# Zeros for the fill of two DRAM tables come from the norm rows' buffer, and one table gets only its extra blocks filled

## The chip, the cores and the metric

The kernel runs on one core of a Trainium2 chip. The metric is the device time of one execution in microseconds (us), smaller being better.

## The reference, cut to what matters

The program is a two-layer encoder on 512 rows of 1024 numbers. Layer 0 mixes tokens with a bidirectional gated DeltaNet, layer 1 with latent attention; each mixer is followed by a layer norm, a mixture of 16 experts of which every token uses two, and another layer norm.

```python
for i in range(DEPTH):
    y = gated_deltanet(x) if i % 2 == 0 else latent_attention(x)
    x = layernorm(ALPHA * x + y, ln1_g[i], ln1_b[i])
    y = grouped_moe(x)        # each token: top 2 experts of its best group
    x = layernorm(ALPHA * x + y, ln2_g[i], ln2_b[i])
```

The change concerns two internal DRAM tables that the expert mixture uses. Each has 26 blocks of 96 rows of 1024 float32: one block for each of the 16 experts, and EXTRA = 10 blocks for tokens that don't fit in an expert's first 96 places.

## The kernel before, in words

The stages run one after the other: the DeltaNet (`delta_net`), the mixture of layer 0, the norm with attention, the mixture of layer 1, the last norm. All engines meet in a barrier between two stages. Within a stage each engine runs its own list of instructions in order, and semaphores tie them.

The DeltaNet goes through 8 head groups ("heads" below, i = 0 to 7). Head 0 is prepared ahead; then one loop body per head does this on the engines: TensorE projects the next head (`wqkv`, the weights of head i+1) while VectorE builds the inverse of a 128x128 triangular matrix per tile (products into `X`, updates of `TU` at L999). Then come the four steps over the chunks of the sequence, in both directions, at L1043 to L1083 (`for st in range(4)`): TensorE makes the chunk's state and output, VectorE takes them over, and TensorE needs VectorE's new state `St` for the next step. In step 0 VectorE copies the first state out of PSUM (L1070) and the first output into `o` (L1079), so `o` is overwritten from here on. After the steps the output is gated and multiplied by `wo`, and added to `res` (L1101).

The sync engine (SP) issues nearly all DMA of this stage, in one list: the first loads, the weights of head 1, the gain and bias rows of two layer norms (`load_rows_of_norm`, into the buffer `gains`, which has a slot for each of two norms, `which % 2`), the router's weights, and then the fill of `slots_x` and `slots_y` with zeros. Then, in a loop, it issues the weights of heads 2 to 7 as buffers come free. The zeros come from a row of 1024 zeros on each of 96 partitions, read once for each block. GpSimd writes them with a memset at the start. In the kernel before they stand in `o`, which VectorE is to overwrite, and so VectorE waits ahead of step 0 until both fills have landed:

```python
zeros = o[0:CAP].rearrange("p t h n -> p (t h n)")
...
dve.wait_ge(zero_filled, 32)
for st in range(4):
```

The mixture writes the rows of its tokens into `slots_x`, each expert reads its block of 96 rows and writes its results, all 96 rows, to its block of `slots_y`. Tokens in extra blocks go the same way, in a branch that runs only if there are any. The norm rows of `which` = 0 are used after the DeltaNet, those of `which` = 1 after the mixture of layer 0.

Of the kernel before, what the change touches and what calls it, by code (L numbers as in the profile page):

```python
# [13 lines left out]
D = 1024  # L14
# [135 lines left out]
def delta_net(nc, t, dram):  # L150
# [10 lines left out]
    with ExitStack() as ctx:  # L161
        def sb(name, shape):
            return ctx.enter_context(nc.sbuf_tensor(name, shape, F32))
# [36 lines left out]
        o = sb("o", [P, TT, 2, P])  # L200
# [31 lines left out]
        zeroed, zero_filled = sem("zeroed"), sem("zero_filled")  # L232
        rs_ready, kq_rs_ready = sem("rs_ready"), sem("kq_rs_ready")
        rs_added, kq_rs_added = sem("rs_added"), sem("kq_rs_added")
        zeros = o[0:CAP].rearrange("p t h n -> p (t h n)")


        earlier = {0: 2, 1: 2, 2: 2, 3: 1, 4: 4, 5: 4, 6: 0, 7: 0}
# [73 lines left out]
        @block.sync  # L312
        def _(sp):
            x_dram = dram["x"][0].rearrange("(t p) n -> p t n", p=P)
            sp.dma_start(ident, dram["const"][:, C_ID:C_ID + P]).then_inc(ident_in, 16)
            for tt in range(TT):
                sp.dma_start(res[:, tt], x_dram[:, tt]).then_inc(t["x_in"][tt], 16)
            sp.dma_start(wba[:], w_dram[:, :, BA_OFF:BA_OFF + 4 * NV]).then_inc(ba_in, 16)
            sp.dma_start(c[:, C_ONE:C_ROW], dram["const"][:, C_ONE:C_ROW]).then_inc(small_in, 16)
            sp.dma_start(bvec[:, 0], dram["dn_a_log"][0].rearrange("d h -> (d h)").partition_broadcast(P)).then_inc(small_in, 16)  # L320
            sp.dma_start(bvec[:, 1], dram["dn_dt_bias"][0].rearrange("d h -> (d h)").partition_broadcast(P)).then_inc(small_in, 16)
            sp.dma_start(nw[:], dram["dn_norm_w"].rearrange("a p -> p a")).then_inc(small_in, 16)

            def load_w(n, late):

                at = (lambda off, w: slice(off, off + w)) if isinstance(n, int) else (lambda off, w: bass.ds(off, w))
                for ct in range(4):
                    off = [n * P, K_OFF + n * P, V_OFF + n * 2 * P, V_OFF + n * 2 * P + P][ct]
                    if late:
                        sp.wait_ge(conv_ready, (n - 1) * 4 + ct + 1)  # L330
                    sp.dma_start(wqkv[:, ct], w_dram[:, :, at(off, P)]).then_inc(w_in[ct], 16)
                if late:
                    sp.wait_ge(taps_ready, n)
                for a, (off, w) in enumerate([(n * P, P), (K_OFF + n * P, P), (V_OFF + n * 2 * P, 2 * P)]):
                    sp.dma_start(tapr[:, a:a + w // P].rearrange("p a b -> p (a b)"), cw_dram[:, at(off, w)]).then_inc(taps_in, 16)

            def load_late(n, late):
                at = (lambda off, w: slice(off, off + w)) if isinstance(n, int) else (lambda off, w: bass.ds(off, w))
                if late:
                    sp.wait_ge(zs_ready, n * 2)  # L340
                sp.dma_start(wz[:], w_dram[:, :, at(Z_OFF + n * 2 * P, 2 * P)]).then_inc(z_in, 16)
                if late:
                    sp.wait_ge(y_ready, 1 + n * 8)
                src = wo_dram[:, at(n * 2, 2), :]
                sp.dma_start(wo[:], src).then_inc(o_in, 16)

            load_w(0, False)
            sp.dma_start(c[:, C_ROW:], dram["const"][:, C_ROW:]).then_inc(rows_in, 16)
            load_late(0, False)
            load_w(1, True)  # L350
            for which in range(2):
                load_rows_of_norm(sp, t, dram, which)
            sp.dma_start(t["router_w"][:], dram["router_w"].rearrange("(k p) e -> p k e", p=P)).then_inc(t["router_in"], 16)
            sp.dma_start(t["router_b"][:], dram["router_bias"].partition_broadcast(P)).then_inc(t["router_in"], 16)

            sp.wait_ge(zeroed, 1)
            for slots in (t["slots_x"], t["slots_y"]):
                blocks = slots.rearrange("(b p) n -> p b n", p=CAP)
                sp.dma_start(blocks, zeros.rearrange("p (a n) -> p a n", a=1).to_broadcast([CAP, BLOCKS, D])).then_inc(zero_filled, 16)
            with sp.Fori(1, NK - 1) as n:  # L360
                load_w(n + 1, True)
                load_late(n, True)
            load_late(NK - 1, True)
            sp.wait_ge(zero_filled, 32)

        @block.tensor
        def _(pe):
# [474 lines left out]
        def _(dve):  # L842
# [130 lines left out]
            def body(i, uses, with_next, per):  # L973
# [63 lines left out]
                    dve.wait_ge(osq_ready, i * 2 + n + 1)  # L1037
                    return nc.vector.tensor_reduce(ss[:, 4 * n:4 * n + 4], sq[:, n].rearrange("p (t m) -> p t m", m=P), AX.X, ALU.add)

                dve.wait_ge(zero_filled, 32)  # L1040
                for st in range(4):
                    for d in range(2):
                        tt = 3 - st if d else st  # L1043
# [73 lines left out]
            with dve.Fori(0, NK - 1) as i:  # L1117
                body(i, MAIN, True, per)
            body(NK - 1, LAST, False, per)


# [23 lines left out]
def load_rows_of_norm(sp, t, dram, which):  # L1145

    gain, bias, layer = NORMS[which]
    sp.dma_start(t["gains"][:, which % 2, 0], dram[gain][layer].partition_broadcast(P)).then_inc(t["gain_in"][which], 16)
    sp.dma_start(t["gains"][:, which % 2, 1], dram[bias][layer].partition_broadcast(P)).then_inc(t["gain_in"][which], 16)
# [93 lines left out]
NE, FF = 16, 256  # L1243
CAP = 96
EXTRA = 2 * SEQ // (CAP + 1)
BLOCKS = NE + EXTRA
# [940 lines left out]
def program(nc, dram, out):  # L2187
    with ExitStack() as ctx:
        t = {
            "const": ctx.enter_context(nc.sbuf_tensor("masks", [P, C_ALL], F32)),  # L2190
            "res": ctx.enter_context(nc.sbuf_tensor("res", [P, TT, D], F32)),
            "xT": ctx.enter_context(nc.sbuf_tensor("xT", [P, KD, SEQ], F32)),
            "ps": [ctx.enter_context(nc.psum_tensor(f"bank{b}", [P, 512], F32)) for b in range(8)],
            "slots_x": nc.dram_tensor("slots_x", (BLOCKS * CAP, D), F32, kind="Internal").ap(),
            "slots_y": nc.dram_tensor("slots_y", (BLOCKS * CAP, D), F32, kind="Internal").ap(),
            "stats": ctx.enter_context(nc.sbuf_tensor("stats", [P, TT, 2, 6], F32)),
            "mla_w_loaded": ctx.enter_context(nc.semaphore("mla_w_loaded")),
            "gains": ctx.enter_context(nc.sbuf_tensor("gains", [P, 2, 2, D], F32)),
            "router_w": ctx.enter_context(nc.sbuf_tensor("router_w_sb", [P, KD, NE], F32)),
            "router_b": ctx.enter_context(nc.sbuf_tensor("router_b_sb", [P, NE], F32)),  # L2200
            "gain_in": [ctx.enter_context(nc.semaphore(f"gain_in_{n}")) for n in range(4)],
            "router_in": ctx.enter_context(nc.semaphore("router_in")),
            "x_in": [ctx.enter_context(nc.semaphore(f"x_in_{n}")) for n in range(TT)],
        }
        delta_net(nc, t, dram)
        mixture(nc, t, dram, 0, 0, "moe0")
        with nc.sbuf_tensor("mla_w_in_sb", [P, KD, QR + KVR + ROPE], F32) as t["mla_w_in"]:
            norm(nc, t, dram, 1, "norm1")
            latent_attention(nc, t, dram)
        mixture(nc, t, dram, 2, 1, "moe1")  # L2210
        norm(nc, t, dram, 3, "norm3", out=out)
# [18 lines left out]
```

## Time and profile before

| | us |
|---|---|
| three runs | 1841.23, 1833.4, 1838.6 |
| median | 1838.6 |
| profiled execution, its own time | 1829.51 |
| its span | 1827.7 |
| PE (TensorE matmul) busy in the span | 1565.5 (86%) |
| DVE (VectorE) busy | 855.6 (47%) |
| ACT (ScalarE) busy | 344.2 |
| POOL (GpSimd) busy | 156.0 |

Times in the trace count from the start of the span. The profiled execution takes 1.81 us more than its span, and is 9.1 us shorter than the median of the three runs. A busy PE is an engine with a matmul in its pipeline, not one at its peak; since stages have different limits, a share over the whole span says little about one stage. PEclk is the clock that TensorE was granted, as a share of full speed.

### The profile page before, as it was taken

The page shows a single profiled execution, that of the slowest core. Times are in us where ns is not written, and L with a number is a line of the kernel's source. Part 1 is how long each engine was busy: PE and PEld are TensorE (multiplying, and loading weights), DVE is VectorE, ACT ScalarE, POOL GpSimd, SP SyncE. Part 2 cuts the span into 40 slices and gives each one's busy share as a digit, 9 for nine tenths or more (in the row PEclk, how much of TensorE's full clock was granted, in tenths as well). Part 3 has the DMA queues.
Part 4 walks back from the last instruction along what each step waited for, and adds up shares of the span by engine and source line. Part 5 has one row for each costly group of instructions (what it writes and reads, how often), then busy time and mean ns, then how long its engine had stood idle before and what let it go on. Part 6 is the DMA issues. An engine that isn't in the chain of part 4 may idle for free. (4 is left out here: it accounts for less than half of the span.)

```text
span 1827.7 us, 20188 instructions
## 1 busy us (share of the span) xinstructions
PE 1565.5 (86%) x6814; PEld 984.1 (54%) x6814; DVE 855.6 (47%) x1758; ACT 344.2 (19%) x765; POOL 156.0 (9%) x143
## 2 busy tenths in 40 slices
PE   8886999989999999999976499956899997399990
PEld 5565586675867758577755244424555554334440
DVE  3653665656656566574555211125155547311115
ACT  2121122231222212222121011101322221011110
POOL 1200201102020020300100100010000000100002
PEclk9998999999999999999985799987899998599995
DMA  6782111111111111100006599942021113669964
GB/s 199 249 256 71 48 35 32 48 35 34 35 46 34 35 43 27 46 0 23 24 1 207 172 325 354 354 149 97 0 83 47 36 35 112 224 212 353 354 226 147
DMA packets 150500, 219.69 MB, mean 120 GB/s; under 512 B 8584, under 2 KB 120448, under 8 KB 150464
## 3 DMA queue, kind: packets, MB, share of 16 engines
q1 hardware_dynamic: 138464, 176.50, 30.2%
q10 hardware_dynamic: 7392, 25.96, 4.1%
q0 software_dynamic: 4608, 16.78, 2.5%
q8 instruction: 20, 0.33, 0.1%
q14 instruction: 16, 0.13, 0.0%
HBM read 175.70 MB, written 43.52 MB: 120 GB/s over the span
## 5 line engine op out<-in xcount | busy, mean ns | idle before, releaser
L1407 PE MATMUL bank<-moe_wgu,moe_xgT 128*96 128x512 f32 x512 | 228.2, 599 | 1.5 <-DVE moe_xgT L1614 1.5
L405 PE MATMUL bank<-xT,wqkv 128*128 128x512 f32 x448 | 210.6, 600 | 0.0
L1407 PEld LDWEIGHTS bank<-moe_wgu,moe_xgT 128*96 128x96 f32 x512 | 81.9, 165 | 123.4 <-issue 123.4
L1614 DVE COPY moe_xgT<-bank 128x384 f32<-128x384 f32 x34 | 19.0, 558 | 226.6 <-PE bank L1398 226.6
L489 PE MATMUL bank<-wz,xT 128*128 128x256 f32 x512 | 117.7, 380 | 0.9 <-DVE res L1101 0.9
L1424 PE MATMUL bank<-moe_wd,moe_hidT 128*96 128x512 f32 x256 | 115.3, 593 | 1.8 <-DVE moe_hidT L1622 1.8
L621 PE MATMUL bank<-wo,oT 128*128 128x512 f32 x256 | 116.0, 603 | 0.8 <-ACT oT L784 0.8
L405 PEld LDWEIGHTS bank<-xT,wqkv 128*128 128x128 f32 x448 | 78.1, 191 | 63.7 <-issue 63.6
L489 PEld LDWEIGHTS bank<-wz,xT 128*128 128x128 f32 x512 | 95.8, 190 | 13.9 <-issue 1.7
L904 DVE SCALAR_TENSOR_TENSOR conv<-bank,taps,conv 128x510 f32<-128x510 f32 (+1 forms) x128 | 95.2, 744 | 8.6 <-ACT conv L673 8.1
L999 DVE TENSOR_TENSOR TU<-TU,bank 128x512 f32<-128x512 f32 x112 | 75.1, 686 | 20.5 <-PE bank L542 12.7
L621 PEld LDWEIGHTS bank<-wo,oT 128*128 128x128 f32 x256 | 48.4, 194 | 56.7 <-issue 55.0
L548 PE MATMUL bank<-W,X 128*128 128x128 f32 x512 | 69.0, 278 | 7.1 <-DVE X L994 6.4
L1101 DVE TENSOR_TENSOR res<-res,bank 128x512 f32<-128x512 f32 x64 | 44.0, 687 | 61.8 <-PE bank L621 61.5
L1460 ACT COPY moe_xgT<-bank 128x384 f32<-128x384 f32 x34 | 16.3, 478 | 292.1 <-PE bank L1398 292.1
L1398 PE MATMUL bank<-masks,moe_x_rows 96*128 96x96 f32 x272 | 29.5, 253 | 48.7 <-DMA moe_x_rows<-slots_x 48.7
L1424 PEld LDWEIGHTS bank<-moe_wd,moe_hidT 128*96 128x96 f32 x256 | 39.2, 163 | 53.3 <-issue 53.3
L548 PEld LDWEIGHTS bank<-W,X 128*128 128x128 f32 x512 | 62.1, 192 | 9.8 <-DVE X L994 9.7
L536 PEld LDWEIGHTS bank<-TU,A 128*128 128x128 f32 x512 | 62.0, 192 | 7.7 <-issue 6.7
L536 PE MATMUL bank<-TU,A 128*128 128x128 f32 x512 | 64.3, 278 | 0.0
L1398 PEld LDWEIGHTS bank<-masks,moe_x_rows 96*128 96x128 f32 x272 | 27.4, 145 | 66.6 <-DMA moe_x_rows<-slots_x 48.9
L1628 DVE COPY moe_y_rows<-bank 96x512 f32<-96x512 f32 x32 | 22.0, 687 | 84.9 <-PE bank L1424 84.9
(298 smaller groups left out, 2418.6 us busy)
## 6 DMA issues: line engine op xcount, KB each, us to landing
moe_wgu<-moe_w_gate SPq DMA_DIRECT2D x32, 1024.0 KB, 10.6
moe_wgu<-moe_w_up SPq DMA_DIRECT2D x32, 1024.0 KB, 13.1
moe_wd<-moe_w_down SPq DMA_DIRECT2D x32, 1024.0 KB, 6.3
wqkv<-dn_w_in SPq DMA_DIRECT2D x32, 512.0 KB, 4.0
moe_x_rows<-slots_x ACTq DMA_DIRECT2D x34, 384.0 KB, 7.2
slots_y<-moe_y_rows ACTq DMA_DIRECT2D x32, 384.0 KB, 6.0
slots_x<-o SPq DMA_DIRECT2D x1, 9984.0 KB, 51.7
slots_y<-o SPq DMA_DIRECT2D x1, 9984.0 KB, 86.8
```

The source lines that it names most:

```text
L405: mm = pe.matmul(bank[:], wqkv[:, ct, k], xT[:, k], start=k == 0, stop=k == KD - 1)
L489: mm = pe.matmul(bank[:, (n % 2) * 256:(n % 2) * 256 + 256], xT[:, k, tt * P:(tt + 1) * P], wz[:, k], start=k == 0, stop=k == KD - 1)
L536: mm = pe.matmul(bank[:, tt * P:(tt + 1) * P], A[:, h, tt], merged(0, h, l, tt), start=True, stop=True)
L548: mm = pe.matmul(bank[:, tt * P:(tt + 1) * P], X[:, h, tt], W[:, h, tt], start=True, stop=True)
L621: mm = pe.matmul(bank[:], oT[:, h, tt], wo[:, h, half * 512:(half + 1) * 512], start=h == 0, stop=h == 1)
L904: ins = nc.vector.scalar_tensor_tensor(out=conv[:, ct, lo:hi], in0=bank[:, lo + d:hi + d], scalar=w[:, j:j + 1], in1=conv[:, ct, lo:hi], o ...
L999: nc.vector.tensor_tensor(merged(which, h, l), merged(which, h, l), change, ALU.subtract).then_inc(U_ready if which else T_ready, 1)
L1101: nc.vector.tensor_tensor(y, y, bank[:], ALU.add).then_inc(y_ready, 1)
L1398: mm = pe.transpose(ps[k // 4][:, k % 4 * CAP:(k % 4 + 1) * CAP], x_rows[:, r, k * P:(k + 1) * P], ident[0:CAP, 0:CAP])
L1407: mm = pe.matmul(ps[2][0:CAP], xgT[:, r, k], wgu[:, r, k].rearrange("p a f -> p (a f)"), start=k == 0, stop=k == KD - 1)
L1424: mm = pe.matmul(ps[4 + half][0:CAP], hidT[:, f], wd[:, r, f, half * 512:(half + 1) * 512], start=f == 0, stop=f == 1)
L1628: nc.vector.tensor_copy(y_rows[:, r, 512:1024], ps[5][0:CAP]).then_inc(y_ready[1], 1)
```

## The change

The row of zeros moves from `o` to the slot of `gains` that holds the bias of norm 1 (`which` = 1). The load of that norm's two rows moves from ahead of the fill to the end of SP's list in this stage, behind the wait for the fill. VectorE's wait for the fill is removed. Of `slots_y` only the 10 extra blocks are filled, not all 26.

```diff
-        zeros = o[0:CAP].rearrange("p t h n -> p (t h n)")
+        zeros = t["gains"][0:CAP, 1, 1]
...
-            for which in range(2):
-                load_rows_of_norm(sp, t, dram, which)
+            load_rows_of_norm(sp, t, dram, 0)
...
             sp.wait_ge(zeroed, 1)
-            for slots in (t["slots_x"], t["slots_y"]):
-                blocks = slots.rearrange("(b p) n -> p b n", p=CAP)
-                sp.dma_start(blocks, zeros.rearrange("p (a n) -> p a n", a=1).to_broadcast([CAP, BLOCKS, D])).then_inc(zero_filled, 16)
+            for rows, n in ((t["slots_x"], BLOCKS), (t["slots_y"][NE * CAP:], EXTRA)):
+                blocks = rows.rearrange("(b p) n -> p b n", p=CAP)
+                sp.dma_start(blocks, zeros.rearrange("p (a n) -> p a n", a=1).to_broadcast([CAP, n, D])).then_inc(zero_filled, 16)
             with sp.Fori(1, NK - 1) as n:
                 load_w(n + 1, True)
                 load_late(n, True)
             load_late(NK - 1, True)
             sp.wait_ge(zero_filled, 32)
+            load_rows_of_norm(sp, t, dram, 1)
...
-                dve.wait_ge(zero_filled, 32)
                 for st in range(4):
```

Two places in the order of instructions show it. The first is SP's list around the fill, from the last tap rows of head 1 to the loop over the later heads. Before:

```order
L335 DMA tapr<-dn_conv_w 5x256
L1148 DMA gains<-ln_g 128x1024
L1149 DMA gains<-ln_b 128x1024
L1148 DMA gains<-ln_g 128x1024
L1149 DMA gains<-ln_b 128x1024
L353 DMA router_w_sb<-router_w 128x8x16
L354 DMA router_b_sb<-router_bias 128x16
L359 DMA slots_x<-o 96x26x1024 [waits zeroed]
L359 DMA slots_y<-o 96x26x1024
L360 UNCONDITIONAL_BRANCH
L360 ISA
L331 ISA [waits conv_ready]
```

And in the changed kernel (its lines from here on are one lower):

```order
L335 DMA tapr<-dn_conv_w 5x256
L1147 DMA gains<-ln_g 128x1024
L1148 DMA gains<-ln_b 128x1024
L352 DMA router_w_sb<-router_w 128x8x16
L353 DMA router_b_sb<-router_bias 128x16
L358 DMA slots_x<-gains 96x26x1024 [waits zeroed]
L358 DMA slots_y<-gains 96x10x1024
L359 UNCONDITIONAL_BRANCH
L359 ISA
L331 ISA [waits conv_ready]
```

Two loads of norm rows are gone from ahead of the fill, the fills read `gains`, and the second has 10 blocks in place of 26. The two loads reappear as the last thing that SP issues in the stage, behind the `wo` of the last head:

```order
L341 DMA wz<-dn_w_in 128x8x256 [waits zs_ready]
L345 DMA wo<-dn_w_out 128x2x1024 [waits y_ready]
L1147 DMA gains<-ln_g 128x1024 [waits zero_filled]
L1148 DMA gains<-ln_b 128x1024
L161 UNCONDITIONAL_BRANCH
```

The second place is VectorE in the loop over the heads, from the last update of `TU` to the first copies of step 0. Before:

```order
L913 SCALAR_TENSOR_TENSOR conv<-th,conv 128x512 [waits th_ready]
L999 TENSOR_TENSOR TU<-TU,bank 128x4x2x64 [waits dn_full3]
L853 REGISTER_ALU [waits zero_filled]
L1070 COPY St<-bank 128x128 [waits dn_full6]
L1070 COPY St<-bank 128x128
L1079 COPY o<-bank 128x256
```

And in the changed kernel:

```order
L913 SCALAR_TENSOR_TENSOR conv<-th,conv 128x512 [waits th_ready]
L999 TENSOR_TENSOR TU<-TU,bank 128x4x2x64 [waits dn_full3]
L853 REGISTER_ALU
L1069 COPY St<-bank 128x128 [waits dn_full6]
L1069 COPY St<-bank 128x128
L1078 COPY o<-bank 128x256
```

The instructions are the same; the wait for `zero_filled` ahead of the first copy is gone, and the wait for TensorE's bank 6 (`dn_full6`) is the only one left there.

## Rows read from the trace of the kernel before

**Rows 1.** The longest waits between 120 and 160 us (time waited, times, longest):

```profile
DVE St L1070 <- DMA slots_y<-o: 27.6, 1, 27.6
PEld bank L574 <- DVE St L1070: 22.6, 1, 22.6
```

**Rows 2.** The timeline of VectorE in head 0 (start, duration, what, idle before):

```profile
68.18 1.22 DVE L960 TENSOR_TENSOR X<-A,masks 128x1024 f32<-128x1024 f32 x1
...
123.08 0.69 DVE L999 TENSOR_TENSOR TU<-TU,bank 128x512 f32<-128x512 f32 x1
151.41 0.70 DVE L1070 COPY St<-bank 128x128 f32<-128x128 f32 x2 [27.64 <-DMA slots_y<-o]
...
161.66 0.60 DVE L1072 SCALAR_TENSOR_TENSOR St<-St,gb,bank 128x128 f32<-128x128 f32 x2 [4.79 <-PE bank L599]
```

**Rows 3.** The same places in head 1, and the start of head 2:

```profile
204.28 1.35 DVE L960 TENSOR_TENSOR X<-A,masks 128x1024 f32<-128x1024 f32 x1
...
259.79 0.69 DVE L999 TENSOR_TENSOR TU<-TU,bank 128x512 f32<-128x512 f32 x1
265.61 0.49 DVE L1070 COPY St<-bank 128x128 f32<-128x128 f32 x2 [5.13 <-PE bank L599]
...
274.13 0.60 DVE L1072 SCALAR_TENSOR_TENSOR St<-St,gb,bank 128x128 f32<-128x128 f32 x2 [4.62 <-PE bank L599]
...
316.76 1.36 DVE L960 TENSOR_TENSOR X<-A,masks 128x1024 f32<-128x1024 f32 x1
```

**Rows 4.** The timeline of TensorE around the first steps of heads 0 and 1:

```profile
128.26 0.61 PE L599 MATMUL bank<-vn,qkd 128*128 128x128 f32 x4
...
152.16 1.22 PE L574 MATMUL bank<-St,kqT 128*128 128x256 f32 x2 [22.41 <-DVE St L1070]
...
204.55 7.13 PE L405 MATMUL bank<-xT,wqkv 128*128 128x512 f32 x16
...
266.29 0.60 PE L574 MATMUL bank<-St,kqT 128*128 128x256 f32 x2
```

**Rows 5.** Windows (core busy times of PE, PEld, DVE, ACT, POOL; clock; DMA share; GB/s):

```profile
130.00:135.00 5.00, 0.00 (x0) 0.00 (x0) 0.00 (x0) 0.00 (x0) 0.00 (x0) 0.98 0.47 176
135.00:150.00 15.00, 0.00 (x0) 0.00 (x0) 0.00 (x0) 0.00 (x0) 0.00 (x0) 0.50 0.32 105
150.00:155.00 5.00, 2.85 (x7) 2.31 (x8) 2.37 (x9) 0.00 (x0) 0.00 (x0) 0.50 0.71 191
155.00:160.00 5.00, 5.00 (x27) 4.33 (x25) 1.52 (x6) 0.36 (x2) 0.00 (x0) 0.97 0.32 90
...
160.00:170.00 10.00, 9.28 (x52) 8.13 (x52) 4.47 (x15) 3.49 (x13) 0.00 (x0) 1.00 0.01 2
...
200.00:400.00 200.00, 192.44 (x989) 139.57 (x989) 124.89 (x250) 44.06 (x98) 24.11 (x20) 1.00 0.13 37
```

**Rows 6.** The issues of the fills, of all DMA issues by tile (KB each, us to landing):

```profile
slots_x<-o SPq DMA_DIRECT2D x1, 9984.0 KB, 51.7
slots_y<-o SPq DMA_DIRECT2D x1, 9984.0 KB, 86.8
```

**Rows 7.** The timeline of SP's queue at the fill and at the stage's end:

```profile
63.63 0.81 SPq L359 DMA_DIRECT2D slots_x<-o  x1
64.49 21.93 SPq L359 DMA_DIRECT2D slots_y<-o  x1
86.80 65.85 SPq L331 DMA_DIRECT2D wqkv<-dn_w_in  x4
...
879.22 0.38 SPq L345 DMA_DIRECT2D wo<-dn_w_out  x1
968.75 0.37 SPq L1330 DMA_DIRECT2D moe_wgu<-moe_w_gate  x1
```

**Rows 8.** Landing of the eight loads into `gains`:

```profile
DMA to landing us min/median/max: 4.9/7.0/9.6
```

**Rows 9.** The first use of the rows of norm 1, in VectorE's timeline:

```profile
1243.54 1.28 DVE L1179 SCALAR_TENSOR_TENSOR res<-res,norm_neg,gains 128x1024 f32<-128x1024 f32 x1
```

## The prediction, made before the changed kernel ran

> **What bounds the kernel now.** I asked first where VectorE's wait for the fill, which the change removes, ends last of all waits. The chain of waits for the stretch around it answers: VectorE's first copy of the state (L1070) waits once, for 27.6 us, for the DMA that fills `slots_y`, and TensorE then waits 22.6 us for that copy [rows 1]. So all compute engines hang on one DMA here. The windows confirm it: from 135 to 150 us no compute engine has any busy time, while DMA has 0.32 of its engines busy and moves 105 GB/s [rows 5]. A fill that is nearly over, with a few of its 16 engines still at it, holds up everything. In the later heads the stage is bound by TensorE: 192.44 of 200 us busy from 200 to 400 us [rows 5].
>
> Next I laid the timelines of VectorE in heads 0 and 1 side by side, since both run the same loop body. Head 1 is the measure of what head 0 would be without the wait [rows 2, 3].
>
> **What the removed wait is worth.** In three pieces.
>
> 1. From the last update of `TU` to the first copy of `St`. Head 0: 151.41 - 123.08 = 28.33 us. Head 1: 265.61 - 259.79 = 5.82 us, of which 5.13 are a wait for TensorE. The difference is 22.51 us. It is not the full 27.64, because the wait for TensorE's bank was hidden behind the fill and appears once the fill is gone: the data of that copy were ready only after the matmuls that start at 128.26 and take 0.61 [rows 4], that is at about 128.87, and 123.08 + 5.82 = 128.90 agrees.
>
> 2. From that copy to the next step's update of the state (L1072). Head 0: 161.66 - 151.41 = 10.25 us; head 1: 274.13 - 265.61 = 8.52 us. Head 0 loses 1.73 us more. The reason stands in the clock: while TensorE stood idle its granted clock fell to 0.50, that is 1.2 GHz, and it was still there when the work came back (0.50 from 150 to 155, 0.97 from 155 to 160 [rows 5]); a group of two matmuls at L574 took 1.22 us in place of 0.60 [rows 4]. Without the idle time this goes too.
>
> 3. Everything behind is the same chain at the same clock (1.00 from 200 to 400 us), so it only starts earlier. As a cross-check, the whole body: head 0 from L960 to L960 is 204.28 - 68.18 = 136.10 us, head 1 is 316.76 - 204.28 = 112.48, a difference of 23.62. The first part of head 0 (68.18 to 123.08, 54.90 us) is 0.61 us shorter than that of head 1 (204.28 to 259.79, 55.51), and 23.62 + 0.61 = 24.23. The sum of pieces 1 and 2 is 22.51 + 1.73 = 24.24 us. This also says that the fill, which runs beside the first part of head 0, costs the engines nothing there: there is no contention to win back.
>
> One rule would give another size to piece 2. By the windows' means (0.98, 0.50, 0.50, 0.97 [rows 5]) the granted clock was at its lower level from about 134.8 to 155.3 us, 20.5 us, of which TensorE worked in little more than 3. The Trainium skill (TensorE: Matmul & The Clock Gate, section "HAM oscillation — how this bites in real kernels") charges the time under the lowered clock times (1 - 1.2/2.4) as extra wall time. Taken as it stands that would make 10.3 us here in place of 1.73, and 32.8 in all. Rows 2 and 3 show 1.73, because the clock was low mostly while nothing ran; I keep 1.73.
>
> **What the other edits cost.** The memset stays one memset of 96x1024 on GpSimd. The two loads of norm 1's rows leave SP's list ahead of the fill, so the fill can start a little earlier, two issues' time. They come back behind the `wo` of head 7, issued at 879.22 by the trace of before, and SP's next work is at 968.75, in the mixture: 89 us of slack for two issues. They must have landed when norm 1 reads them at 1243.54 [rows 9], 360 us later; a load of such rows lands in at most 9.6 us [rows 8]. All this is hidden, at a cost of nothing; the cover goes only if SP reaches them more than 350 us late. Their wait for the fill is met some 700 us before. The 1 MB that they bring moves from a stretch of full DMA to an empty one.
>
> The shorter fill: 9984 + 3840 = 13,824 KB in place of 19,968 KB [rows 6], 0.69 of it. The two together took from 63.63 to 64.49 + 86.8 = 151.3 us, 87.7 us. If the slowest DMA engine keeps its pace, the new fill ends at 63.6 + 0.69 x 87.7 = 124 us. If instead the first fill still ends at 63.63 + 51.7 = 115.3 and the second needs 10/26 of the 36 us left, at 129 us. No compute engine waits for it any more, so the end matters only for what is queued behind it: SP's loads of `wqkv` for head 2. They kept SP from 86.80 to 152.65, the first of the four waiting for room behind the fill [rows 7], and had landed by 160, since DMA is empty from there on (0.01, 2 GB/s, from 160 to 170 [rows 5]). Their first use is at 204.55 in TensorE's list [rows 4], and comes 24.2 us earlier now, at 180.3. Even with the old landing there would be 20 us to spare; with the new fill they land by about 137, as much behind its end as before. Cost nothing. Hence the cut of `slots_y` by itself adds nothing to the gain of the moved source, though without the moved source it would bring most of it, since 124 to 129 is about where TensorE's bank is ready, 128.9.
>
> **The sum.** 24.24 us off the profiled execution: span 1827.7 to 1803.5, own time 1829.51 to 1805.3. Off the median of the runs shown, 1838.6: **1814.4 us**, a ratio of 0.987. The median is 9.1 us above the profiled execution and the runs are 7.8 us apart, so the level is less certain than the difference. A difference of 0.5%, 9.2 us, is about the least that a measurement of this kernel can tell from no change.
>
> **The rivals.**
>
> *The wait is longer in the runs than in the profile.* The fill's end hangs on the slowest DMA engine, and nothing else in the kernel has engines wait for a transfer for so long. If all of the 9.1 us between profile and median are a longer tail of the fill, the gain is 33.3 us and the time 1805.3. For it: the DMA share falls so low in the tail that a small slowdown of one engine moves the end. Against it: the two mixtures and the start also hang on DMA, and the excess can be theirs. Chance 0.13. The clock rule taken as it stands gives nearly the same time by another way: 1838.6 - 32.8 = 1805.8, if 20.5 us of work ran at half speed. TensorE shows no instruction at all from 135 to 150 [rows 5], so this gets a chance of 0.02.
>
> *Something else holds step 0.* If VectorE or TensorE were held near 151 us by another wait that the fill's wait covers, the time would stay at 1836 to 1840. The order shows just one wait left ahead of the copy, that for bank 6, and TensorE had written it by 128.87. For the result to be within 0.5%, that bank would have to come 15 us later. Chance 0.03.
>
> *Slower: head 2's weights.* SP's queue is in order, and behind the fill stand the weights that TensorE needs at the start of head 1's body. If they landed after 204.55 the kernel would be slower by just the excess; to be slower by 0.5% they would have to land after 213.7. They had landed by 160 with 6,144 KB more ahead of them. The price is one us for each us of delay, the point of decision is 53 us beyond the old landing. Chance 0.02, other surprises included.
>
> **How the numbers follow.** The likeliest case, with chance 0.80, is 1814.4 us; with piece 2 lost or a scatter of the median of some 4 us its own range is 1809 to 1820. The range for 8 in 10 reaches down to the longer-tail case, whose 0.15 it takes in, and gives up some of the upper scatter: 1804 to 1821. Faster by over 0.5% (below 1829.4): 0.80 + 0.15 = 0.95. Within 0.5%: 0.03. Slower: 0.02.
>
> **What would show it right or wrong.** The first copy of `St` in head 0 should start near 128.9 us, with some 5 us of idle time before it put down to TensorE. The next update should follow after 8.5 us, not 10.3, with the clock at 1.00 through 120 to 160 us. Head 0's body should take about 112 us. The wait for `slots_y` should be gone from VectorE's list, the last fill should land between 124 and 129 us, TensorE should not wait for `wqkv` of head 2 at about 180, and norm 1 should not wait for `gains`. All stages from the mixture on should look as before, 24 us earlier. A gain far from 24 us in the trace would make piece 1 or 2 wrong; a gain of 24 there and of 33 in the medians would speak for the longer tail.

## The result, and the profile after

The changed kernel took 1808.46 us (median of 4 runs, 1803.69 to 1810.14) against 1837.78 us for the kernel before (4 runs, 1833.4 to 1841.23). The ratio is 0.9837, with a 95% interval of 0.9808 to 0.9867. It is faster by 1.6%, or 29.3 us between the medians. In the two profiled executions the spans are 1827.7 and 1805.3 us, which is only 22.4 us. So the two measures of one change differ by 7 us, and the experiments below look for them.

First VectorE's timeline of the changed kernel at the places of [rows 2] and [rows 3], heads 0 and 1 (lines past L1040 are one lower than before):

```profile
66.37 1.22 DVE L960 TENSOR_TENSOR X<-A,masks 128x1024 f32<-128x1024 f32 x1
...
121.47 0.69 DVE L999 TENSOR_TENSOR TU<-TU,bank 128x512 f32<-128x512 f32 x1
127.30 0.49 DVE L1069 COPY St<-bank 128x128 f32<-128x128 f32 x2 [5.13 <-PE bank L599]
...
135.82 0.61 DVE L1071 SCALAR_TENSOR_TENSOR St<-St,gb,bank 128x128 f32<-128x128 f32 x2 [4.62 <-PE bank L599]
...
178.46 1.36 DVE L960 TENSOR_TENSOR X<-A,masks 128x1024 f32<-128x1024 f32 x1
...
290.94 1.35 DVE L960 TENSOR_TENSOR X<-A,masks 128x1024 f32<-128x1024 f32 x1
```

The first copy of `St` now starts 5.83 us after the last update of `TU` (28.33 before), waits 5.13 us for TensorE, and the next update of the state follows after 8.52 us (10.25 before). These two spans are those of head 1 to 0.01 us. The body of head 0 takes 112.09 us in this execution (113.6 to 113.8 in three others, see piece 3 below), and that of head 1 112.48 as before.

TensorE and the clock at the same place, as a timeline and as a window (busy times of PE, PEld, DVE, ACT, POOL; clock; DMA share; GB/s), to be held against [rows 4] and [rows 5]:

```profile
127.53 0.61 PE L599 MATMUL bank<-vn,qkd 128*128 128x128 f32 x4
127.97 0.60 PE L574 MATMUL bank<-St,kqT 128*128 128x256 f32 x2
```

```profile
125.00:145.00 20.00, 18.92 (x108) 16.61 (x106) 8.85 (x32) 5.52 (x19) 0.00 (x0) 1.00 0.06 18
```

The 22 us of idle time between these two groups of matmuls are gone, the second takes 0.60 us in place of 1.22, and the granted clock stays at 1.00 (2.4 GHz).

SP's queue and the fills, for [rows 7] and [rows 6]:

```profile
57.16 0.63 SPq L353 DMA_DIRECT2D router_b_sb<-router_bias  x1
57.83 1.23 SPq L358 DMA_DIRECT2D slots_x<-gains  x1
59.10 25.02 SPq L358 DMA_DIRECT2D slots_y<-gains  x1
84.50 37.97 SPq L331 DMA_DIRECT2D wqkv<-dn_w_in  x4
...
853.88 0.46 SPq L1147 DMA_DIRECT2D gains<-ln_g  x1
854.39 0.43 SPq L1148 DMA_DIRECT2D gains<-ln_b  x1
```

```profile
slots_x<-gains SPq DMA_DIRECT2D x1, 9984.0 KB, 38.8
slots_y<-gains SPq DMA_DIRECT2D x1, 3840.0 KB, 61.9
```

The last fill lands at 59.1 + 61.9 = 121.0 us (121.3 to 122.5 in the other three executions), and the two loads of norm 1's rows are issued at 854 us, 367 us ahead of the norm.

### The profile page after: what moved, and what is told of

Same layout as the page of the kernel before. It is cut to its first block and busy times, and to the rows that moved or that the text cites. A ratio compares the mean times of both kernels' runs of the same rounds, so it can differ in the third digit from the quotient of the medians.

```text
span 1805.3 us, 20186 instructions
## 1 busy us (share of the span) xinstructions
PE 1565.8 (87%) x6814; PEld 985.1 (55%) x6814; DVE 854.9 (47%) x1758; ACT 344.2 (19%) x765; POOL 157.1 (9%) x143
## 5 line engine op out<-in xcount | busy, mean ns | idle before, releaser
L405 PEld LDWEIGHTS bank<-xT,wqkv 128*128 128x128 f32 x448 | 78.1, 191 | 63.7 <-issue 63.6
L999 DVE TENSOR_TENSOR TU<-TU,bank 128x512 f32<-128x512 f32 x112 | 75.1, 686 | 20.5 <-PE bank L542 12.8
L621 PEld LDWEIGHTS bank<-wo,oT 128*128 128x128 f32 x256 | 48.1, 193 | 56.1 <-issue 54.5
L1100 DVE TENSOR_TENSOR res<-res,bank 128x512 f32<-128x512 f32 x64 | 44.0, 688 | 60.9 <-PE bank L621 60.6
## 6 DMA issues: line engine op xcount, KB each, us to landing
moe_wgu<-moe_w_up SPq DMA_DIRECT2D x32, 1024.0 KB, 13.1
```

The lines of the kernel that those rows point to most:

```text
L405: mm = pe.matmul(bank[:], wqkv[:, ct, k], xT[:, k], start=k == 0, stop=k == KD - 1)
L621: mm = pe.matmul(bank[:], oT[:, h, tt], wo[:, h, half * 512:(half + 1) * 512], start=h == 0, stop=h == 1)
L999: nc.vector.tensor_tensor(merged(which, h, l), merged(which, h, l), change, ALU.subtract).then_inc(U_ready if which else T_ready, 1)
L1100: nc.vector.tensor_tensor(y, y, bank[:], ALU.add).then_inc(y_ready, 1)
```

## The experiments

Twelve runs were made: the two halves of the change, more fill with and without the wait, the kernel before and the changed kernel three more times each, and two other places in the buffer to read the zeros from. In the runs that compare times, the medians of the kernel before were 1834.9 to 1837.7 us.

**Only the source moved** (`e1_source_only`). The changed kernel, but `slots_y` filled whole:

```diff
-            for rows, n in ((t["slots_x"], BLOCKS), (t["slots_y"][NE * CAP:], EXTRA)):
+            for rows, n in ((t["slots_x"], BLOCKS), (t["slots_y"], BLOCKS)):
```

> The zeros move and the wait is removed, but slots_y is still filled whole. If the removed wait is the whole cause, this is as fast as the changed kernel: about 1808 us, ratio 0.984, first copy of St near 128 us, with the fill landing as before near 151 us and nobody waiting for it. If the gain came from moving 6 MB less (traffic beside the computation), this stays near the kernel before, at a ratio of 0.99 to 1.00. If head 2's weights behind the long fill matter, TensorE waits for them near 180 us and part of the gain is lost; I expect no such wait.

Measured: 1806.48 us, ratio 0.983 (0.9807 to 0.9852), the whole gain. The fill landed at 60.6 + 88.6 = 149.2 us and nobody waited for it:

```profile
128.21 0.49 DVE L1069 COPY St<-bank 128x128 f32<-128x128 f32 x2 [5.13 <-PE bank L599]
```

```profile
60.61 24.07 SPq L358 DMA_DIRECT2D slots_y<-gains  x1
85.06 65.56 SPq L331 DMA_DIRECT2D wqkv<-dn_w_in  x4
150.72 1.84 SPq L335 DMA_DIRECT2D tapr<-dn_conv_w  x3
```

SP was held as long as before (65.56 us) and could issue the last of head 2's weights only by 150.6 us, but TensorE's first use of them came at 181.33 without a wait. The theory that the 6 MB themselves cost time falls.

**Only the size cut** (`e2_size_only`). The kernel before, its wait and its source kept:

```diff
-            for slots in (t["slots_x"], t["slots_y"]):
+            for rows, n in ((t["slots_x"], BLOCKS), (t["slots_y"][NE * CAP:], EXTRA)):
```

> The zeros stay in VectorE's output buffer and VectorE still waits for the fill, but only 10 blocks of slots_y are filled. In the changed kernel the last fill landed at 121.0 us; with two more loads ahead it should land at 122 to 126 here, before TensorE's bank is ready at about 129. So the wait costs nothing: about 1808 to 1811 us, ratio 0.984 to 0.986. If the last engine's tail is longer than that, the first copy of St starts later than 129 us by just the excess.

Measured: 1810.28 us, ratio 0.9847 (0.9824 to 0.987), nearly all of the gain too. The fill landed at 64.01 + 62.6 = 126.6 us, a little later than I expected and 2.6 us before the copy, which again waited for TensorE alone:

```profile
129.18 0.49 DVE L1070 COPY St<-bank 128x128 f32<-128x128 f32 x2 [5.13 <-PE bank L599]
```

```profile
64.01 22.22 SPq L359 DMA_DIRECT2D slots_y<-o  x1
```

```profile
slots_y<-o SPq DMA_DIRECT2D x1, 3840.0 KB, 62.6
```

So either half of the change does the work of both, as far as the overlapping intervals can tell. The cut alone has a margin of only 2.6 us, though, while the moved source has no wait to be late for.

**More fill behind the wait** (`e3_more_fill`). The kernel before, with 10 more blocks in the second table (they are never used):

```diff
-            for slots in (t["slots_x"], t["slots_y"]):
+            for rows, n in ((t["slots_x"], BLOCKS), (t["slots_y"], 36)):
...
-            "slots_y": nc.dram_tensor("slots_y", (BLOCKS * CAP, D), F32, kind="Internal").ap(),
+            "slots_y": nc.dram_tensor("slots_y", (36 * CAP, D), F32, kind="Internal").ap(),
```

> The kernel before, with its wait, and a table slots_y that is 10 blocks longer (36) and filled whole. If the wait on the slowest DMA engine sets the time, the end of the fill and the whole kernel come later by 10/26 of the 36 us between the two landings, 14 us: about 1851 us. If the fill's end is set by the total rate of some 320 GB/s, 3.9 MB more cost 12 us. If the bytes are hidden, no change.

Measured: 1847.62 us, ratio 1.0054 (1.0035 to 1.0074), 9.9 us slower than the kernel before in the same comparison, where 14 were expected. The chain of waits from 120 to 170 us (time waited, times, longest):

```profile
DVE St L1070 <- DMA slots_y<-o: 44.3, 1, 44.3
PEld bank L574 <- DVE St L1070: 39.2, 1, 39.2
```

The wait is 44.3 us, 16.7 more than in [rows 1] but 13.1 more than its mean over four executions of the kernel before (below). The mechanism holds and more fill is paid for. The price of 9.9 to 13 us (6.4 to 13.6 by the interval of the ratio) is nearest to the second of the two rates that were named, 12 us, but these runs can't rule out 14 with certainty.

**More fill without the wait** (`e4_fill_long_no_wait`). The changed kernel, but with a second table of 78 blocks, filled whole:

```diff
-            for rows, n in ((t["slots_x"], BLOCKS), (t["slots_y"][NE * CAP:], EXTRA)):
+            for rows, n in ((t["slots_x"], BLOCKS), (t["slots_y"], 78)):
...
-            "slots_y": nc.dram_tensor("slots_y", (BLOCKS * CAP, D), F32, kind="Internal").ap(),
+            "slots_y": nc.dram_tensor("slots_y", (78 * CAP, D), F32, kind="Internal").ap(),
```

> The changed kernel without VectorE's wait, but slots_y has 78 blocks and is filled whole: 39.9 MB of fill in place of 13.8. This tests the rival in which head 2's weights queue behind the fill. At the pace of the kernel before (19,968 KB in 87.7 us) the fill ends at 58 + 175 = 233 us, and the weights land some 6 to 15 us later, while TensorE needs them at 178.7: it waits 55 to 70 us, 1865 to 1880 us in all. If weights could pass the fill, the time would stay at 1808 us.

Measured: 1857.49 us, 49.0 more than the changed kernel (ratio to the kernel before 1.0114, 1.0087 to 1.0142). SP's queue and TensorE at the start of head 1's body:

```profile
59.71 24.00 SPq L358 DMA_DIRECT2D slots_y<-gains  x1
84.10 137.72 SPq L331 DMA_DIRECT2D wqkv<-dn_w_in  x4
221.91 1.49 SPq L335 DMA_DIRECT2D tapr<-dn_conv_w  x3
```

```profile
226.61 1.86 PE L413 MATMUL bank<-masks,tapr 5*128 5x5 f32 x8 [45.85 <-DMA tapr<-dn_conv_w]
228.40 9.24 PE L405 MATMUL bank<-xT,wqkv 128*128 128x512 f32 x16
```

The fill landed at 59.7 + 160.3 = 220 us, 13 earlier than I had scaled it, and SP could issue head 2's loads and taps only then. TensorE waited 45.85 us for the taps, the last of them, and lost about 3 more at the lowered clock (9.24 us for a group that takes 7.13 in [rows 4], 1.86 for one that took 1.05 in the changed kernel): 48.8 of the 49.0. So the rival in which head 2's loads queue behind the fill is a real mechanism. In the change it has no effect, since they land well before 178 us.

**The kernel before, three more times** (`before_again1` to `3`), for the 7 us between the two measures.

> The kernel before, unchanged, once more. If the longer runs of it (1833 to 1841 us against 1829.5 in the profiled one) come from the tail of the fill, the landing of slots_y (151.3 us in the first profile) moves with the time of the execution, one us for one. If they come from elsewhere (the clock's steps in the mixtures, the start), the landing stays within 1 or 2 us of 151 and the later stages differ.

> The same, to have a third execution: same expectation as for the second.

> The same, to have a fourth execution: same expectation as for the second.

VectorE's first copy in the three traces, in this order, one each:

```profile
153.25 0.70 DVE L1070 COPY St<-bank 128x128 f32<-128x128 f32 x2 [29.02 <-DMA slots_y<-o]
```

```profile
157.02 0.70 DVE L1070 COPY St<-bank 128x128 f32<-128x128 f32 x2 [33.33 <-DMA slots_y<-o]
```

```profile
159.08 0.70 DVE L1070 COPY St<-bank 128x128 f32<-128x128 f32 x2 [34.70 <-DMA slots_y<-o]
```

| execution | wait for the fill | copy at | span |
|---|---|---|---|
| the one of [rows 2] | 27.64 | 151.41 | 1827.7 |
| `before_again1` | 29.02 | 153.25 | 1829.6 |
| `before_again2` | 33.33 | 157.02 | 1833.7 |
| `before_again3` | 34.70 | 159.08 | 1840.1 |

For the first three the span follows the wait one for one: 1.4 and 5.7 us more wait, 1.9 and 6.0 us more span. In the fourth, 7.1 us more wait explain 7.1 of 12.4 us; another 3 lie in the attention stage (299.45 us from its first load to the next mixture's first, 296.42 in the first), and most of the rest elsewhere in the DeltaNet. So the wait in the profile I predicted from was the shortest of four, 3.5 us under their mean of 31.17.

**The changed kernel three more times** (`after_again`, `after_look2`, `after_look3`). The first was timed in five rounds:

> The changed kernel, unchanged, timed in more rounds. If the gain is that of the trace, 24.2 us, the ratio comes down to about 0.987; if the runs of before have a longer tail of the fill, it stays at 0.982 to 0.984.

Measured: 1805.88 us, ratio 0.9856 (0.9837 to 0.9875), 29.0 us between the medians. The interval reaches up to the 0.987 of the trace alone; the ratios of both comparisons lie below it. The spans of the four executions are 1805.3, 1804.1, 1804.9 and 1804.0 us, 1804.6 on average, those of the kernel before 1832.8 on average. That is 28.2 us. The changed kernel's four spans are 1.3 us apart where the others' were 12.4, but the timed runs don't bear out that the scatter has gone with the wait: in this comparison five of the changed kernel lie between 1805.33 and 1811.54 us, and nine of the kernel before between 1830.61 and 1837.69.

The other two are single executions, for a difference in the first mixture that is told below:

> The changed kernel, unchanged. The first mixture, from its first load to the load behind it, took 273.7 to 274.1 us in the executions where the engines had stood still in the DeltaNet, and 276.4 to 276.6 us in four of five without that. If this is chance, both lengths turn up here and in the next run; if the missing idle time costs these 2.5 us as a rule, both are near 276.5 us and after_again was the exception.

> The same as for after_look2, for a fourth execution of the changed kernel.

Measured: 274.3 and 274.0 us from SP's first load of the mixture to the load behind it. With 273.8 in `after_again` three of four executions of the changed kernel have the short length, and `e6_source_0_to_63`, in which the engines stood still for 45 us, has a long one (277.0). So no rule ties the long one to the missing idle time. Whether it is more frequent without idle time stays open: it came in one of seven executions with a standstill in the DeltaNet, and in four of seven without.

**The zeros read from other partitions** (`e5_source_32_to_95`, `e6_source_0_to_63`). One question was still open: why does a fill of 20.4 MB move over 300 GB/s with all DMA engines busy up to 115 us, and then need another 36 us with fewer and fewer of them (0.74 busy from 115 to 125 us, 0.32 from 135 to 150)? Both kernels are the kernel before, with its wait and the same bytes, and differ from each other only in the rows of `o` that are read:

```diff
-        zeros = o[0:CAP].rearrange("p t h n -> p (t h n)")
+        zeros = o[32:96].rearrange("p t h n -> p (t h n)")
...
-                blocks = slots.rearrange("(b p) n -> p b n", p=CAP)
-                sp.dma_start(blocks, zeros.rearrange("p (a n) -> p a n", a=1).to_broadcast([CAP, BLOCKS, D])).then_inc(zero_filled, 16)
+                blocks = slots.rearrange("(b p) n -> p b n", p=64)
+                sp.dma_start(blocks, zeros.rearrange("p (a n) -> p a n", a=1).to_broadcast([64, BLOCKS * CAP // 64, D])).then_inc(zero_filled, 16)
...
-            nc.gpsimd.memset(zeros, 0.0).then_inc(zeroed, 1)
+            nc.gpsimd.memset(o[:], 0.0).then_inc(zeroed, 1)
```

This is the edit for 32 to 95; the other has `o[0:64]` in its first line and is the same in the rest.

> The kernel before with both tables filled whole and with VectorE's wait, but the zeros are read from partitions 32 to 95 in place of 0 to 95, in 39 blocks of 64 rows; the bytes are the same. In the kernel before DMA moved 319 to 331 GB/s with all engines busy up to 115 us, and then a few engines needed 36 us more. If the tail comes from how the source's partitions spread over the paths that the DMA engines read them by, this spread is even and the 20.4 MB go at some 320 GB/s: the fill ends near 127 us and the time falls to 1808 to 1812 us. If the tail comes from the destination or from single engines, it ends near 151 to 159 us and the time stays at 1830 to 1840 us. By the Trainium skill (SBUF — State Buffer, section on Door 1: the DMA port swizzle), partitions 0 to 63 are reached by one half of the DMA ports and 64 to 127 by the other, which is the first of the two cases.

> The same with the zeros read from partitions 0 to 63. If the source's partitions make the tail, this spread is the worst: all bytes take the paths that two thirds took before. The slowest share of before took 87.7 us or more for two thirds of the bytes, so the fill would take up to 1.5 times as long, 115 to 131 us, end at 178 to 195 us, and the time rise to 1860 to 1880 us. If the source doesn't matter, the time stays at 1830 to 1840 us.

Measured: 1806.05 us for partitions 32 to 95, ratio 0.9833 (0.9816 to 0.9849), and 1850.26 us for 0 to 63, ratio 1.0076 (1.0057 to 1.0095). The window from 80 to 100 us, columns as above, in the kernel with 32 to 95, in that with 0 to 63, and in the kernel before:

```profile
80.00:100.00 20.00, 19.59 (x104) 13.16 (x103) 13.05 (x25) 6.64 (x12) 0.00 (x0) 1.00 1.02 419
```

```profile
80.00:100.00 20.00, 19.59 (x104) 13.16 (x103) 12.87 (x25) 6.41 (x11) 0.00 (x0) 1.00 0.98 201
```

```profile
80.00:100.00 20.00, 19.59 (x104) 13.13 (x103) 13.05 (x26) 6.41 (x11) 0.00 (x0) 1.00 1.01 329
```

419, 201 and 329 GB/s, with all DMA engines busy in each. With 32 to 95 the second fill landed at 63.7 + 54.5 = 118.2 us, ahead of the copy at 127.72, and with 0 to 63 the copy waited for them until 168.52:

```profile
slots_y<-o SPq DMA_DIRECT2D x1, 9984.0 KB, 54.5
```

```profile
168.52 0.70 DVE L1070 COPY St<-bank 128x128 f32<-128x128 f32 x2 [45.49 <-DMA slots_y<-o]
```

The source's partitions set the rate. My sizes were off in both. For the even spread I expected 320 GB/s, the fill's end near 127 us and 1808 to 1812 us, and got 419, 118.2 and 1806.05. For the uneven one I expected a fill of 115 to 131 us and 1860 to 1880 us, and it took 104 us (its second table landed 103.4 us after its issue) and 1850.26. The rule of the Trainium skill that the expectation named (SBUF — State Buffer, section "Door 1: The DMA port swizzle (why `[64,N]` ≈ `[32,N]`)"), by which 0 to 63 reach only half of the DMA ports, agrees with the two rates, 201 being 0.48 of 419. By that rule the 96 partitions of the kernel before put two thirds of the bytes on one half of the ports. That fits a fill that starts fast and ends slowly, but not its length: two thirds of 20.4 MB at the 201 GB/s measured for 0 to 63 would take 68 us (an estimate from these rows), the fill took 87.7, and its tail moved 105 GB/s [rows 5]. No run shows which engines or partitions the tail belongs to, so its last part stays open.

## Why the prediction was right, point by point

**Piece 1, the removed wait.** Right in mechanism, and in size for the profile it was read from: predicted 22.51, measured 28.33 - 5.83 = 22.50 us between the two profiles. The wait for TensorE's bank that I said would appear is there, 5.13 us. Mis-sized as a forecast of the medians: the wait is 27.64 us in [rows 1] and 31.17 us on average over four executions, so the piece is worth some 26 us on average (from the last update of `TU` to the copy 31.9 us before and 5.8 after, means of four executions each).

**Piece 2, the clock.** Predicted 1.73, measured 10.25 - 8.52 = 1.73 us, and 1.8 to 2.3 against the other three executions of the kernel before. The trace sides with the rows, not with the formula of the Trainium skill (TensorE: Matmul & The Clock Gate, section "HAM oscillation — how this bites in real kernels") applied to all 20.5 us at the lowered clock, which would have made 10.3. Of these 20.5 us TensorE worked in 3.15, and half of that is 1.6, near the 1.73.

**Piece 3, nothing behind changes.** Right for the DeltaNet in the first profile, not quite in the others. In the first, the copy itself comes 24.1 us earlier, and everything in the DeltaNet from the next update of the state on 25.8 us earlier (head 2 at 290.94 in place of 316.76). That is 24.2 and a further 1.6 that the profiled execution gained at the very start: a group of 16 projections took 7.13 us in it and 8.83 in the other, which is the clock again (1.00 against 0.72 from 20 to 26 us).

In the other three executions of the changed kernel head 0 gives some of this back. From that update of the state to the start of head 1's body they take 44.1 to 44.3 us, where all four executions of the kernel before and the first of the changed one take 42.6. TensorE at the place where they part, in `after` (the first execution) and in `after_again`:

```profile
158.60 1.09 PE L607 MATMUL bank<-masks,zs 128*128 128x128 f32 x8 [2.51 <-DVE zs L1092]
159.53 1.88 PE L448 MATMUL bank<-triG,masks 128*128 128x512 f32 x4
```

```profile
159.44 1.97 PE L607 MATMUL bank<-masks,zs 128*128 128x128 f32 x8 [2.50 <-DVE zs L1092]
161.20 2.51 PE L448 MATMUL bank<-triG,masks 128*128 128x512 f32 x4
```

Both stood idle for 2.5 us; then the granted clock was 1.00 in the first (158 to 162 us) and 0.57 in the second (159 to 163 us). The six executions whose engines had stood still for the fill (four of the kernel before, `e3_more_fill`, `e6_source_0_to_63`) all took 42.6 us for this stretch. Of the eight others two took 42.6 (`after`, `e2_size_only`) and six 44.1 to 44.3 (`e4_fill_long_no_wait` among them, whose standstill comes only behind this stretch). So the changed kernel loses 1.2 us here on average over its four executions, a cost that piece 3 put at nothing. It came only where no standstill lay ahead of it; why the clock falls there is not shown.

In the first mixture about 3 us were given back. TensorE's first two large groups there, before and after:

```profile
1029.31 8.69 PE L1407 MATMUL bank<-moe_wgu,moe_xgT 128*96 128x512 f32 x16 [0.74 <-DVE moe_xgT L1614]
...
1041.26 7.03 PE L1407 MATMUL bank<-moe_wgu,moe_xgT 128*96 128x512 f32 x16
```

```profile
1004.37 9.87 PE L1406 MATMUL bank<-moe_wgu,moe_xgT 128*96 128x512 f32 x16 [0.74 <-DVE moe_xgT L1613]
...
1017.66 8.31 PE L1406 MATMUL bank<-moe_wgu,moe_xgT 128*96 128x512 f32 x16
```

The clock came back later in that execution: 1.18 and 1.28 us in these two groups. The change doesn't bring it about each time, as the other executions show. From the first load of the mixture to the load behind it the first execution of the changed kernel takes 276.4 us, its other three 273.8 to 274.3, and the four of the kernel before 273.9 to 274.1. Hence the 22.4 us between the two spans are 24.2, plus 1.6 at the start, less the 3 that were given back around this mixture.

**The fill's new end.** Predicted 124 to 129, measured 121.0. Its length, 63.2 us from the issue of the first fill, is 2.5 more than scaling by the bytes gave (60.7). The start was earlier than I allowed, 57.83 in place of 63.63: 1.6 us of it come from the stage's start, some 1.2 from the two issues, and 3.1 from SP's issue of the router's bias, which took 0.63 us in place of 3.69 with 1 MB less ahead of it. It costs and gains nothing, as said, but for the cut alone these few us decide whether it waits.

**The other edits.** Hidden, as predicted: the moved loads at 854 us, no wait for `gains` at norm 1, none for head 2's weights. `e4_fill_long_no_wait` shows that the last was worth naming as a condition.

**The likeliest case and the rivals.** The forecast of 1814.4 took the first profile's wait as that of every run. The first rival said that the runs' wait is longer, by all of the 9.1 us between the profile and the median. The truth lies between: on average 3.5 us longer. So the number was helped by the width of the range. The measured 1808.46 is 6 us below the forecast and 0.5 us below the 1809 to 1820 that the likeliest case had as its own; it lies in 1804 to 1821 because that range reached down for this rival.

The means of four executions each, 28.2 us apart, come apart into 26.0 for the wait and 1.9 for the clock behind it, less the 1.2 that the rest of head 0 gave back; 1.3 by the end of head 0's first part, which is mostly TensorE's clock at the start of the kernel; and 0.1 in all stages behind head 0 together (0.7 more in the attention, 0.6 less in the first mixture). The last two are differences between executions that nobody forecast, and the medians of the timed runs, 29.3 and 29.0 us apart, are a little more still; the interval of the first comparison, 24.4 to 35.3 us, holds the 28.2. The rivals of no change and of a slower kernel had no part in it.

## What to carry to other kernels

A wait that protects a buffer from being overwritten is worth the idle time beyond the next wait that it hides, not its own length: 22.5 of 27.6 us here, and the untouched next round of the same loop gives that number beforehand. The wait on this long transfer differed more from execution to execution (27.6 to 34.7 us) than any later stage of the kernel (by at most 3.3 us), so take it from several profiles before you put a number on removing it. And before you cut or move a fill from SBUF, look at which partitions it reads: the second fill landed 103 us after its issue from partitions 0 to 63 and 55 us from 32 to 95.

## What the runs showed of the hardware that I had not expected

- The rate of a fill from SBUF to DRAM by 16 busy DMA engines was 201 GB/s from partitions 0 to 63, 419 from 32 to 95, and 329 from 0 to 95, which fell to 105 GB/s with 0.32 of the engines busy [rows 5].
- The same fill of 20.4 MB landed 86.8, 87.7, 92.7 and 93.0 us after its second issue in four executions of the same program.
- With the same instructions ahead of it, TensorE's clock came back at different moments after an idle time: the first mixture took 273.7 to 274.3 us in nine executions and 276.4 to 277.0 in five, of kernels that are alike there. In the one of `after`, most of the excess was a longer stay at 1.2 GHz in the first large groups of matmuls after a wait.
- After the same 2.5 us of idle time in head 0 TensorE's granted clock was 1.00 in one execution of the changed kernel (158 to 162 us) and 0.57 in another (159 to 163 us), which cost 1.5 us.
